# A fused transformer trunk step: modulation in column groups, mostly in the merge, and heads that start on chunks of h

## The reference, cut to what matters

```
mod = silu(cond) @ w_ada + b_ada              # 2 conditions x 6144: sh1 sc1 g1 sh2 sc2 g2
h   = rmsnorm(x, norm1) * (1 + sc1) + sh1
x_in, bg, cg, q, zf, zb, iv, og, ga, gb = split(h @ w_in)
ya  = (bg * conv3(cg * x_in)) @ w_out_a
ob, S = bidirectional_recurrence(q, zf, zb, iv, og)   # 8 heads
mix = (sigmoid(ga) * ya + sigmoid(gb) * (ob @ w_out_b)) @ w_o
x   = x + g1 * mix
h2  = rmsnorm(x, norm2) * (1 + sc2) + sh2
x   = x + g2 * expert_choice_ffn(h2)          # 16 experts; then a final rmsnorm
```

## Time and profile before

| what | value |
|---|---|
| median of 3 runs | 2586.36 us (2585.72 to 2588.29) |
| the profiled execution, its own time | 2586.46 us |
| its span, first to last instruction | 2584.7 us |
| PE busy | 2426.2 us (94% of the span) |
| weight loads on PE busy | 2294.1 us |
| DVE, ACT, POOL busy | 1025.5, 841.2, 366.6 us |
| HBM read and written | 330.82 and 43.55 MB, 145 GB/s over the span |
| mean granted TensorE clock | 0.971 |

### The profile page before, as it was taken

One profiled execution on the slowest core, in us unless ns is written; L12 is line 12 of the kernel. 1 busy time (PEld: TensorE's weight loads), 2 busy tenths in 40 slices (PEclk: granted clock), 3 DMA queues, 4 the chain that ended last, 5 costly groups with the idle time before them and its releaser, 6 DMA issues. The chain is left out here.

```text
span 2584.7 us, 47081 instructions
## 1 busy us (share of the span) xinstructions
PE 2426.2 (94%) x17645; PEld 2294.1 (89%) x17645; DVE 1025.5 (40%) x2630; ACT 841.2 (33%) x1989; POOL 366.6 (14%) x611
## 2 busy tenths in 40 slices
PE   7799999999999999999799989669999999999992
PEld 2499999999999999999799978369999999999992
DVE  2455453645455453645433344732222122222222
ACT  2454544454454544454322022111111111111112
POOL 0011110211111110211101124110101010101011
PEclk9899999999999999999999999879999999999996
DMA  7412112121212112121354234738877887788754
GB/s 277 171 44 63 51 52 64 37 78 30 77 44 62 51 52 64 37 79 30 98 205 151 73 118 141 274 98 291 280 242 255 290 276 244 257 291 280 237 190 163
DMA packets 368200, 375.95 MB, mean 145 GB/s; under 512 B 11803, under 2 KB 340539, under 8 KB 368096
## 3 DMA queue, kind: packets, MB, share of 16 engines
q1 hardware_dynamic: 353928, 326.58, 37.8%
q0 software_dynamic: 14160, 47.81, 6.5%
q10 hardware_dynamic: 10, 0.02, 0.0%
HBM read 330.82 MB, written 43.55 MB: 145 GB/s over the span
## 5 line engine op out<-in xcount | busy, mean ns | idle before, releaser
L717 PE MATMUL bank<-HT,W 128*128 128x384 f32 x5760 | 1047.9, 338 | 9.9 <-DVE bank L1214 9.9
L717 PEld LDWEIGHTS bank<-HT,W 128*128 128x128 f32 x5760 | 995.4, 188 | 13.3 <-DVE bank L1214 10.2
L2016 PE MATMUL bank<-XET,WEA 128*128 128x144 f32 x4096 | 511.2, 287 | 0.6 <-DVE XET L2088 0.6
L2016 PEld LDWEIGHTS bank<-XET,WEA 128*128 128x128 f32 x4096 | 505.9, 191 | 1.2 <-issue 0.7
L2031 PE MATMUL bank<-HID,WED 128*128 128x144 f32 x2048 | 257.8, 287 | 0.0
L2031 PEld LDWEIGHTS bank<-HID,WED 128*128 128x128 f32 x2048 | 252.6, 190 | 0.7
L1409 PE MATMUL bank<-YO,W 128*128 128x384 f32 x960 | 172.7, 337 | 19.2 <-ACT YO L1425 19.2
L1409 PEld LDWEIGHTS bank<-YO,W 128*128 128x128 f32 x960 | 169.0, 190 | 19.5 <-issue 19.5
L2047 ACT ACTIVATE SG<-bank 128x144 f32<-128x144 f32 x128 | 37.3, 291 | 409.5 <-PE bank L2016 409.5
L2117 DVE TENSOR_TENSOR GU<-SG,bank 128x144 f32<-128x144 f32 x128 | 39.0, 304 | 300.4 <-ACT SG L2051 300.4
L2055 ACT ACTIVATE YT<-bank 128x144 f32<-128x144 f32 x128 | 37.3, 291 | 274.3 <-PE bank L2031 274.3
(11 more groups left out here) (218 smaller groups left out, 2795.9 us busy)
## 6 DMA issues: line engine op xcount, KB each, us to landing
WEA<-in_w_e_gate_dram SPq DMA_DIRECT2D x64, 1024.0 KB, 5.1
WEA<-in_w_e_up_dram SPq DMA_DIRECT2D x64, 1024.0 KB, 10.5
WED<-in_w_e_down_dram SPq DMA_DIRECT2D x64, 1024.0 KB, 9.9
W_FULL<-in_w_in_dram SPq DMA_DIRECT2D x80, 512.0 KB, 3.7
AW<-in_w_ada_dram SPq DMA_DIRECT2D x10, 2048.0 KB, 9.1
sg_d<-QR SPq DMA_DIRECT2D x48, 192.0 KB, 1.9
GL<-sg_d POOLq DMA_DIRECT2D x48, 192.0 KB, 2.7
ya_d<-CY SPq DMA_DIRECT2D x24, 192.0 KB, 1.9
```

Source lines behind the costliest of these rows:

```text
L717: ins = nc.tensor.matmul(bank[:, 0:CH], W[:, slot, a, k, :], HT[:, b, k, at * CH:(at + 1) * CH], start=(i == 0 and k == 0), stop=(i == 2 a ...
L2016: ins = nc.tensor.matmul(PS[2 * s + f % 2][:, 0:NX], WEA[:, 4 * s + f // 2, k, (f % 2) * P:(f % 2 + 1) * P], XET[:, k, :], start=(k == 0), ...
```

## The change

Of the twelve blocks of the modulation only the first four stay ahead of the heads. They have a buffer each, so that all their loads are issued at once, and each matmul of 512 columns becomes four of 128 columns, whose two output rows lie at partitions 0, 32, 64 and 96 of one bank; bias and norm are laid out the same way, one addition and one multiplication serve all four blocks, and 4 transposes of 128x128 take the place of 16. The x tiles are transposed and copied to `HT_FULL` without scale and shift, two or three tiles between the blocks. When scale and shift are there (`mod_ct`), DVE and ACT apply them in place, chunk by chunk, and split each chunk. The barrier between opening and heads goes: the opening's streams run ahead of the heads' in the same block, and the first three product steps wait for their own chunk alone.

The other 4,096 columns of w_ada (g1, sh2, sc2, g2) are made in the merge: 16 blocks of 256 columns, 1,024 KB each, in one buffer `AM` in the unused fifth weight slot, reloaded as soon as PE has read it; per block 8 x 4 matmuls of 64 columns in the four output bands, after the first product step of each weight block (`mod_rows`). DVE adds the bias, ACT issues the stores to `mod_d`. PE's and DVE's loops of the merge are written out. The end of the mix stage and the start of the experts' lose the g2 work.

The core of the diff:

```diff
-        AW = pro("AW", [P, 2, KT, 512])
-        MODR = pro("MODR", [2, 6 * D])
-        NR = pro("NR", [2, 2, D])
+        AW = pro("AW", [P, 4, KT, 512])
+        BIX = pro("BIX", [P, 4, P])
+        NIX = pro("NIX", [P, 2, P])
+        MODX = pro("MODX", [P, 4, P])
...
+        def opening_sync(sp):
...
+            sp.dma_start(AW[:, 0], w_ada_v[:, :, 0:512]).then_inc(ada_in[0], 16)
+            sp.wait_ge(rows_zero, 2)
+            for j in range(4):
+                sp.dma_start(BIX[32 * j:32 * j + 2],
+                             b_ada[0, 0:2 * D].rearrange("(b j i) -> j b i", j=4, i=P)[j].partition_broadcast(2)) \
+                  .then_inc(rows_in, 16)
...
+            for b in range(1, 4):
+                sp.dma_start(AW[:, b], w_ada_v[:, :, b * 512:(b + 1) * 512]).then_inc(ada_in[b], 16)
+            for slot, off in enumerate((ZF, ZB, IV)):
+                wload(sp, slot, w_in_v, off)
...
+        def opening_act(act):
...
+                if t > 0:
+                    src, dst = normal_rows(t - 1, 1)
+                    act.wait_ge(xt_t, 2 * t)
+                    nc.scalar.activation(dst, src, ACT.Copy).then_inc(xt_act, 1)
...
+            high(0)
+            act.wait_ge(mod_ct, 1)
+            act.sem_inc(gate_read, 6)
+            for n in range(NCH):
+                cols = slice(n * CH, (n + 1) * CH)
+                for k in range(4, KT):
+                    for lo_, hi_, c in chunk_parts(n):
+                        h = HT_FULL[:, 1, k, lo_:hi_]
+                        ins = nc.scalar.activation(h, h, ACT.Identity, bias=SH1T[:, k, c:c + 1],
+                                                   scale=A1T[:, k, c:c + 1])
+                ins.then_inc(full_act, 1)
+                act.wait_ge(full_dve, n + 1)
+                nc.scalar.activation(HT[:, 0, 0:4, cols], HT_FULL[:, 1, 0:4, cols], ACT.Copy).then_inc(h_hi, 1)
+                act.wait_ge(full_act, n + 1)
+                nc.scalar.activation(HT[:, 0, 4:KT, cols], HT_FULL[:, 1, 4:KT, cols], ACT.Copy).then_inc(h_hi, 1)
+                if n < 2:
+                    high(1 + n)
...
+        def opening_tensor(pe):
+            def ada(b):
+
+                pe.wait_ge(ada_in[b], 16)
                 for k in range(KT):
+                    for j in range(4):
+                        ins = nc.tensor.matmul(PS[1][32 * j:32 * j + 2, b * P:(b + 1) * P], CT[:, k, :],
+                                               AW[:, b, k, j * P:(j + 1) * P],
                                                start=(k == 0), stop=(k == KT - 1))
+                ins.then_inc(ada_mm, 1)
...
+            t = 0
+            for b, n in enumerate((2, 3, 3, 1)):
+                ada(b)
+                for i in range(n):
+                    rows(t)
+                    t += 1
+            pe.wait_ge(mod_fix, 2)
+            for b in range(4):
+                ins = nc.tensor.transpose(PS[3][:, b * P:(b + 1) * P], MODX[:, b, :], IDENT)
+            ins.then_inc(mod_t, 1)
+
+        def opening_vector(dve):
...
+            dve.wait_ge(rows_in, 128)
+            dve.wait_ge(ada_mm, 4)
+            nc.vector.tensor_tensor(MODX[:].rearrange("p b i -> p (b i)"), PS[1][:],
+                                    BIX[:].rearrange("p b i -> p (b i)"), ALU.add).then_inc(mod_fix, 1)
+            dve.wait_ge(mod_fix, 1)
+            nc.vector.scalar_tensor_tensor(MODX[:, 2:4], MODX[:, 2:4], 1.0, NIX[:],
+                                           ALU.add, ALU.mult).then_inc(mod_fix, 1)
...
+            for n in range(NCH):
...
+                ins.then_inc(full_dve, 1)
+                if n == 0:
+                    low(0)
+                for half in range(2):
+                    ks = slice(4 * half, 4 * half + 4)
+                    dve.wait_ge(h_hi, 2 * n + half + 1)
+                    nc.vector.tensor_tensor(HT[:, 1, ks, cols], HT_FULL[:, 1, ks, cols],
+                                            HT[:, 0, ks, cols].bitcast(F32), ALU.subtract).then_inc(h_lo, 1)
+                if n < 2:
+                    low(1 + n)
...
+                opening_sync(sp)
...
-                            if last:
+                            if last and slot < 4:
                                 wload(sp, slot, w_oa_v, slot * P)
...
+                    first = g == 0 and kind == "f"
+                    if first:
+                        pe.wait_ge(h_hi, 2 * at + 2)
...
                     for i, (a, b) in enumerate(PARTS):
+                        if first and b == 1:
+                            pe.wait_ge(h_lo, 2 * at + 2)
...
+        AM = nc.alloc_sbuf_tensor_at("AM", [P, KT, GW], F32, offset=W_OFF + 4 * SLOT)
...
+        def mod_weights(eng, b):
+
+            eng.dma_start(AM[:], w_ada_v[:, :, 2 * D + b * GW:2 * D + (b + 1) * GW]).then_inc(am_in, 16)
...
+                    if p == 0:
+                        mod_weights(sp, 0)
+                sp.wait_ge(bi_zero, 1)
...
                 for b in range(4, NB):
 
+                    sp.wait_ge(am_mm, b - 3)
+                    mod_weights(sp, b - 3)
                     sp.wait_ge(m_product, (b - 3) * NCH)
                     wload(sp, b % 4, w_oa_v if b < KT else w_ob_v, (b % KT) * P)
...
+                def mod_rows(b):
+
+                    pe.wait_ge(am_in, 16 * b + 16)
+                    if b >= 2:
+                        pe.wait_ge(am_row, b - 1)
+                    for k in range(KT):
+                        for j in range(4):
+                            ins = nc.tensor.matmul(PS[4 + b % 2][32 * j:32 * j + 2, 0:64], CT[:, k, :],
+                                                   AM[:, k, 64 * j:64 * j + 64],
+                                                   start=(k == 0), stop=(k == KT - 1))
+                    ins.then_inc(am_mm, 1)
...
+                                if n == 0:
+                                    mod_rows(p * KT + 4 * s + m)
...
+                    for j in range(4):
+                        act.dma_start(mod_d[:, v, :].rearrange("c (b j i) -> j c b i", j=4, i=64)[j],
+                                      BI[32 * j:32 * j + 2, 4 * v:4 * v + 4]).then_inc(g2_out if v == 3 else mod_out, 16)
...
+                    if b == 0:
+                        dve.wait_ge(bi_in, 128)
+                    dve.wait_ge(am_mm, b + 1)
+                    nc.vector.tensor_tensor(BI[0:98, b], PS[4 + b % 2][0:98, 0:64], BI[0:98, b],
+                                            ALU.add).then_inc(am_row, 1)
...
-                        sp.dma_start(AWG[:], w_ada_v[:, :, b * 512:(b + 1) * 512]).then_inc(awg_in, 16)
...
-                dve.wait_ge(bg2_in, 16)
-                for i in range(2):
-                    dve.wait_ge(g2_mm, i + 1)
...
-                sp.dma_start(mod_d[:, 3, :], MG[:]).then_inc(g2_out, 16)
-                sp.wait_ge(g2_out, 16)
```

More of the change, by code:

```diff
@@ L174, in trunk @@
         cond_in = sem("cond_in")
+        rows_zero = sem("rows_zero")
         rows_in = sem("rows_in")
         lbi_in = sem("lbi_in")
-        ada_in = [sem(f"ada_in{i}") for i in range(2)]
+        ada_in = [sem(f"ada_in{i}") for i in range(4)]
         x_in_s = [sem(f"x_in{i}") for i in range(2)]
@@ L209, in wload @@
             eng.dma_start(W_FULL[:, slot, 1], src[:, :, ds(col, P)]).then_inc(weights_in[slot], 16)
-        def evac_h(eng, t, half):
-            c = 0 if t == CTX else 1
-            eng.wait_ge(mod_ct, 1)
-            eng.wait_ge(ht_t, 2 * t + half + 1)
-            for k in range(4 * half, 4 * half + 4):
-                out = HT_FULL[:, 1, k, t * P:(t + 1) * P]
-                src = PS[4 + half + 2 * (t % 2)][:, (k % 4) * P:(k % 4 + 1) * P]
-                if half == 0:
-                    ins = nc.vector.tensor_scalar(out, src, A1T[:, k, c:c + 1],
-                                                  SH1T[:, k, c:c + 1], ALU.mult, ALU.add)
-                else:
-                    ins = nc.scalar.activation(out, src, ACT.Identity, bias=SH1T[:, k, c:c + 1],
-                                               scale=A1T[:, k, c:c + 1])
-            ins.then_inc(ht_act if half else ht_dve, 1)
@@ new lines, in opening_vector, with low @@
+            nc.vector.scalar_tensor_tensor(MODX[:, 2:4], MODX[:, 2:4], 1.0, NIX[:],
+                                           ALU.add, ALU.mult).then_inc(mod_fix, 1)
+            dve.wait_ge(mod_t, 1)
+            for dst, lo_ in ((SH1T, 0), (A1T, 256)):
+                ins = nc.vector.tensor_copy(dst[:], PS[3][:, lo_:lo_ + 256].rearrange("p (k r) -> p k r", r=32)[:, :, 0:2])
+            ins.then_inc(mod_ct, 1)
+            def low(slot):
+                dve.wait_ge(w_hi, slot + 1)
+                nc.vector.tensor_tensor(W[:, slot, 1], W_FULL[:, slot, 1],
+                                        W[:, slot, 0].bitcast(F32), ALU.subtract).then_inc(w_lo, 1)
@@ new lines, in opening_vector @@
+            dve.wait_ge(mod_ct, 1)
+            for n in range(NCH):
+                cols = slice(n * CH, (n + 1) * CH)
+                for k in range(4):
```

(33 more changed lines are left out.)

386 lines of the change are left out of this document (163 added, 223 removed).

## The result

The changed kernel takes **2558.68 us** (median of 4 runs, 2558.03 to 2559.57) against 2586.04 for the kernel before, measured beside it (4 runs, 2585.47 to 2588.29): 27.4 us less, ratio 0.989 with a 95% interval of 0.9874 to 0.9906. The forecast was 2555.5.

What follows compares the result with a forecast made beforehand. PE was taken to bound heads, merge and experts, with its modulation streaming on the opening's path. Opening -51, merge blocks +19, loads +2, mix stage's addition -1.3 sum to -31: 2586.46 to 2555.5 us, range 2545 to 2573.

Steps and rivals of the forecast that it cites:

- the two limits of some 43 us for the fourth block: Opening: loads of 13.4 MB (42 us) and the x tiles' chain (some 43); the fourth block's matmuls taken to start at 42.
- landed near 42: Opening: sign of being right in the new profile, the fourth w_ada block landed near 42 us.
- The ping-pong between DVE and ACT: Opening's chunks: DVE waits 1.4 us for ACT's high half, so a chunk takes 7.8 us, more than the product's 4.16.
- +21.9 to +26.2: Opening: the third product's start and end after `mod_ct`, in us, so ready at 76.7 instead of 128.18.
- The unused slot's load goes, hidden: Last head: the load of the unused weight slot goes, but is hidden, so no time was forecast for it.
- a wait for the first block alone: Merge: sign of being right, PE waits 1 to 2 us for the first modulation block's load and no other.
- A: Merge and opening: only two bands run at once, 2.1 us per merge block; 2573.5 us, chance 0.18 with milder forms.
- B: Merge and opening: bands run one after another, 3.9 us per merge block; slower than before, 2606 us, chance 0.05.
- C: Opening: `mod_ct` at 58 to 62, or longer DVE and ACT blocking per chunk; 2565 us, chance 0.17 with E.
- E: Opening: a second cause delays the first products; third ready at 85 to 90, sum -18 to -23, chance 0.17 with C.
- the main case: Whole kernel: the predicted 2555.5 us, between 2548 and 2562, with the third product ready at 76.7; chance 0.50.
- D: Merge: transfers collide and a late block stalls PE each time, 1 us each, +16; 2571 us, chance 0.07.

Runs made afterwards that it cites:

- a_xgate: a_xall, but POOL issues x tiles 2 to 8 only once the first w_ada block has landed, and PE's tile order is 2, 3, 4, 0; 2555.43 us.
- a_best: The kernel after with a_xgate, a_order, 16 of a_warm's fillers and another order of scaling and splitting weights and chunks; 2543.11 us.
- a_best2: a_best with only PE's fixed order of the x tiles changed, 2, 5, 2, 0 instead of 2, 3, 4, 0; 2539.82 us.
- a_warm: The kernel after with 24 extra matmuls into an unused bank in PE's pause between the second and third product; 2556.01 us.
- b_slot: The kernel before with one edit: the last head no longer loads the weight slot the merge does not use; 2584.83 us against 2588.47.
- a_order: The kernel after with ob's chunks issued one by one behind the merge's first weight loads and modulation matmuls after the second product of a weight block; 2554.11 us.
- a_oneband: The kernel after with the merge's 64 modulation matmuls per block all in one output band, so most modulation rows are bias only; 2597.32 us.
- a_open: a_xall plus high weights on ACT ahead of `mod_ct`, low weights on POOL, next chunk scaled before the last's low half, tiles 3, 3, 3, 0; 2552.77 us.
- a_xall: The kernel after with a place of its own for each of the nine x tiles and all their loads issued at once; 2555.87 us.

## Why the prediction was right, point by point

**The sum.** The forecast was 3.2 us too low. The mechanisms came out as worked out, but the closeness is partly luck: the opening fell 3.1 us short, the merge cost 2.7 more than forecast and the end of the kernel 1.3, while the seam gave 2.9 that nobody had forecast and the mix stage 1.3 more than its term.

**Bound.** Right. Each microsecond of PE work in the merge cost its own time, and the modulation's streaming in the opening was on the path.

**`mod_ct`.** 51.5 against 50.5. The blocks took 3.58 cold and 1.93 warm (3.5 and 1.8 in the working). Of the two limits of some 43 us for the fourth block only one was there. The transfers were taken at the 343 GB/s of the earlier trace rows; they ran at 409 to 415 from 12 to 30 us, and the block had landed at 34.4, so this sign of being right (landed near 42) did not come. Its start, 44.55 against 42, was set by the chain of the x tiles and by their place in PE's order, which a_xgate, a_best and a_best2 then moved: with both changed it starts at 38.05. The working of the x chain alone was enough to give the right time.

**Chunks.** The ping-pong between DVE and ACT is as described: the third product starts 21.9 us after `mod_ct`, the number of the working. The error is the term behind it, "+21.9 to +26.2", which took 4.2 to 4.3 us for that product as if PE were warm. It paused 4.29 us before it, the granted clock was at 0.66, and it took 6.9; a_warm gave back 2.2 to 2.4 of this 2.7. ACT's four scalings took 2.50 instead of 1.8: in the first chunk that put the first product at 5.5 us after `mod_ct` instead of 4.8, in the second and third it was hidden, for there ACT waited for DVE.

**The unused slot.** "The unused slot's load goes, hidden" is the step that was wrong. The load was hidden from PE, but the barrier waits for the store behind it in SP's queue: 2.9 us, by b_slot. It made up for most of the opening's shortfall, by luck.

**The merge.** A block adds 1.22 us against the 1.2 of the working: 64 x 14 ns of full overlap, and 0.3 for the changes of mode. By the 60 cycles for each matmul that "TensorEngine Tiling (Array Packing)" of the Trainium skill states in section Instruction Overhead, a block would be 1.6 us or more, an estimate from that figure; 13.5 ns from one instruction's start to the next, in different bands, do not agree with it. The waits were 3.9 us against 2: the first as worked out (1.29 against 1.5), the second 2.10 against 0.5. For that one the working looked at the transfers of ob; in fact SP issued it only at 1264.21, 7.5 us after PE had freed the buffer, being at the issues of ob and of eight bias rows till then. The sign of a wait for the first block alone did not come either. 16 x 1.22 = 19.5 for the blocks and 3.9 for the waits make 23.4 of the 23.7; in a_order, without a wait, it is 19.5 of 19.8.

**The mix stage.** PE's freed matmuls gave nothing, as said, and the addition went: 1.2 us by PE's wait for `CUM`, against 1.3.

**Rivals.** A (2.1 us for a block) and B (3.9) are refuted by the 1.22 us of a block; a_oneband shows B's 3.7 us when there is one band. C and E: the third product was ready at 80.3, later than the main case's 76.7, but by less than C or E would have it (E wanted 85 to 90). D, a late block each time, did not occur: three waits in sixteen blocks.

## What to carry to other kernels

When an operand with two rows streams through PE, cut it into column groups and put them in different output bands: here 64 instructions took 1.07 us instead of 3.73, and it paid though nothing hid the blocks in the merge. When work moves out of a stage's start, look next at the fixed order of the engine that takes its inputs: which tile stands behind which transfer was worth 7 us at the third product and 3 to 6 us of the time here. And a load that nobody uses is not free if a store that a barrier waits for is issued behind it.

## What the runs showed of the hardware that was not expected

- 64-column fp32 matmuls with two output rows: 55.7 ns from one start to the next in one band (a_oneband), 13.5 ns over four (the kernel after), each 219 ns long in both.
- DVE's 128x384 scalings of fp32 in place took 0.41 to 0.47 us each in the kernel after. Beside POOL's 128x1024 subtractions, which took 2.3 to 2.5 us each, two of eight took 1.38 and 2.90 and ended just after a subtraction did; eight took 6.54 us instead of 3.42 (a_open, a_best). "GPSIMD Engine Reference" of the Trainium skill, section Specifications, says that GpSimd's SBUF interfaces are shared with VectorE; the run agrees.
- After a pause of 4.3 us on PE, which followed 4.4 us of work, a product began at a granted clock of 0.50 (1.2 GHz) and took 6.9 us, at 0.66 on average from 70 to 80 us; with the pause filled the clock was 1.00 and the product took 4.5 (a_warm).
- Seven more x loads delayed the first w_ada block by 8.7 us, though SP issued that block at 2.7 us, while POOL was issuing the nine x loads from 1.4 to 6.3 on its own queue (a_xall). The rate from 12 to 22 us was 414 GB/s, against 409 in the kernel after; the bytes of both came at once.
